# Two heads of a state scan's tail, shifted against each other on TensorE, with quarters of other products between them

## What is computed

```
def step(state, inp):
    r_t, w_t, k_t, v_t, a_t, b_t = inp
    sa = jnp.einsum('bhvk,bhk->bhv', state, a_t)
    state = (state * w_t[:, :, None, :] + sa[..., None] * b_t[:, :, None, :]
             + v_t[..., None] * k_t[:, :, None, :])
    return state, jnp.einsum('bhvk,bhk->bhv', state, r_t)
```

## Time and profile before

| what | value |
|---|---|
| median of 3 runs | 4059.29 us (4054.79 to 4061.07) |
| the profiled execution's own time | 4055.24 us |
| its span, first to last instruction | 4053.5 us |
| mean granted clock of PE | 0.975 of 2.4 GHz |
| PE busy | 3873.0 us, 28244 instructions |
| DVE, ACT, POOL busy | 1954.3, 1635.8, 1652.3 us |
| the sixteen pairs | from some 80 to 512 us and from some 1397 to 1830 us of the span |

### The profile page before, as it was taken

The page is one execution under the profiler, slowest core; times in us unless marked ns, Lnnn a source line. Parts: engine busy times, 40 slices in busy tenths (PEclk is TensorE's granted clock), DMA queues, the critical chain, the costliest instruction groups (busy, mean ns, idle before and its releaser), DMA issues. The chain is left out here.

```text
span 4053.5 us, 67108 instructions
## 1 busy us (share of the span) xinstructions
PE 3873.0 (96%) x28244; PEld 3167.8 (78%) x28244; DVE 1954.3 (48%) x3042; ACT 1635.8 (40%) x2723; POOL 1652.3 (41%) x902
## 2 busy tenths in 40 slices
PE   8999989999999899998899999989999999999998
PEld 6888867878887788886787888777878887787887
DVE  7777673246534777767324654436231123523112
ACT  5554444343334555444434333446233224523222
POOL 4444412434445444441243444534444444444443
PEclk9999999989999899999998999989999999999999
DMA  3111113325532211111332554221222322122332
GB/s 134 48 49 44 67 45 112 104 99 188 186 131 98 85 48 49 44 68 44 111 99 97 193 183 135 99 73 43 98 89 99 98 90 79 53 94 89 99 99 83
DMA packets 108731, 379.52 MB, mean 94 GB/s; under 512 B 12561, under 2 KB 12945, under 8 KB 107793
## 3 DMA queue, kind: packets, MB, share of 16 engines
q1 hardware_dynamic: 98208, 357.27, 25.9%
q10 hardware_dynamic: 10224, 17.97, 1.2%
HBM read 359.46 MB, written 15.73 MB: 93 GB/s over the span
## 5 line engine op out<-in xcount | busy, mean ns | idle before, releaser
L293 POOL TENSOR_TENSOR Wlo<-raw,Whi 128x1024 fp32r<-128x1024 f32 x552 | 1334.4, 2420 | 1995.2 <-ACT Whi L280 1995.0
L228 PE MATMUL ps<-hh,Whi 128*128 128x512 f32 x2864 | 1152.1, 402 | 27.9 <-DVE hl L377 10.1
L228 PE MATMUL ps<-hl,Whi 128*128 128x512 f32 x2864 | 1123.4, 392 | 0.0
L228 PE MATMUL ps<-hh,Wlo 128*128 128x512 f32 x2864 | 1123.2, 392 | 0.0
L280 ACT ACTIVATE Whi<-raw 128x1024 fp32r<-128x1024 f32 x552 | 581.8, 1055 | 708.9 <-PE ps L228 607.9
L228 PEld LDWEIGHTS ps<-hh,Whi 128*128 128x128 f32 x2864 | 542.7, 189 | 160.2 <-issue 28.3
L228 PEld LDWEIGHTS ps<-hl,Whi 128*128 128x128 f32 x2864 | 543.1, 190 | 116.7 <-issue 8.6
L228 PEld LDWEIGHTS ps<-hh,Wlo 128*128 128x128 f32 x2864 | 542.2, 189 | 115.8
L228 PE MATMUL ps<-gh,Whi 128*128 128x512 f32 x864 | 337.6, 391 | 3.8 <-POOL Wlo L293 3.8
L228 PE MATMUL ps<-gh,Wlo 128*128 128x512 f32 x864 | 336.2, 389 | 0.0
L228 PE MATMUL ps<-gl,Whi 128*128 128x512 f32 x864 | 336.1, 389 | 0.0
(11 more groups left out here) (363 smaller groups left out, 5913.6 us busy)
## 6 DMA issues: line engine op xcount, KB each, us to landing
raw<-in_stream SPq DMA_DIRECT2D x554, 512.0 KB, 3.5
ada<-in_ada SPq DMA_DIRECT2D x96, 512.0 KB, 4.6
park_x<-xT SPq DMA_DIRECT2D x2, 2048.0 KB, 7.3
park_yh<-yh ACTq DMA_DIRECT2D x16, 256.0 KB, 2.1
park_yl<-yl ACTq DMA_DIRECT2D x16, 256.0 KB, 2.3
xT<-park_x SPq DMA_DIRECT2D x2, 2048.0 KB, 8.8
yrh<-park_yh ACTq DMA_DIRECT2D x16, 256.0 KB, 8.0
yrl<-park_yl ACTq DMA_DIRECT2D x16, 256.0 KB, 7.9
```

What stands on the lines that cost most here:

```text
L228: last = pe.matmul(ps, left[a](k), right[c](k), start=start and k == 0 and i == 0, stop=stop and k == n - 1 and i == 2)
L293: pool.tensor_tensor(b["Wlo"][:, slot], b["raw"][:, raw_slot(b, u)], b["Whi"][:, slot].bitcast(F32), SUB) \
```

## The change

In the tail, head 1 comes one step behind head 0: U0; then U1 with Z0, block by block; then Z1 with L0, block by block; then L1. Between them stand quarters of r's and k's products: r's last quarter behind U0, and k's first three behind the two mixed groups and behind L1. k's last quarter stays behind S3, and behind S2 there is none. In the inverse, r's first three quarters stand one each behind levels 1, 2 and 3. ACT copies r's result in the tail, between the copies of U0 and U1, and no longer behind level 2. On DVE the state updates S2 and S3 come straight behind RY0 and RY1, and both copies of y behind them. No product is added or dropped, and shapes stay as they are.

```diff
-TAIL_V = Steps("M10", "M11", "M20", "M21", "RY0", "YL0", "RY1", "S2", "YL1", "S3", "Y")
+TAIL_V = Steps("M10", "M11", "M20", "M21", "RY0", "S2", "RY1", "S3", "YL0", "YL1", "Y")
...
+    def u_part(h, c):
+        for u in range(2):
+            last = pe.matmul(b["ps"][half(u), BANK_U + h, c * P:(c + 1) * P], b["XT"][half(u), h, block(c)],
+                             b["AG"][half(u), c, h], start=c == 0, stop=u == 0, skip_group_check=True)
+        if c == BLK - 1:
+            last.then_inc(s["tail_p"], 1)
+
+    def z_part(h, c):
+        last = pe.matmul(b["ps"][half(1), BANK_Z + h, c * P:(c + 1) * P], b["TB"][half(0), h, c, 0, CB:P],
+                         b["Wm"][half(0), h, c], start=True, stop=True)
+        if c == BLK - 1:
+            last.then_inc(s["tail_p"], 1)
+
+    def l_part(h, c):
+        last = pe.matmul(b["ps"][half(1), BANK_U + h, c * P:(c + 1) * P], b["XT"][half(1), h, block(c)],
+                         b["Zs"][half(1), h, c * P:(c + 1) * P], start=False, stop=True, skip_group_check=True)
+        if c == BLK - 1:
+            last.then_inc(s["tail_p"], 1)
+
+    pe.wait_ge(s["tail_a"], TAIL_A(p, "GV"))
+    pe.wait_ge(s["inv_v"], INV_V(p, f"T{LEVELS - 1}0"))
+    for c in range(BLK):
+        u_part(0, c)
+    if p + 2 < PAIRS:
+        rwkv_gemm_pe(pe, s, b, ring, p + 2, "r", 3, 4)
+    else:
+        early_query_pe(pe, s, b, ring, FILL[p, "r"], 3, 4)
+    pe.wait_ge(s["inv_v"], INV_V(p, f"T{LEVELS - 1}1"))
+    pe.wait_ge(s["tail_a"], TAIL_A(p, "U0"))
+    for c in range(BLK):
+        u_part(1, c)
+        z_part(0, c)
+    ahead(0)
+    pe.wait_ge(s["tail_a"], TAIL_A(p, "Z0"))
+    for c in range(BLK):
+        z_part(1, c)
+        l_part(0, c)
     ahead(1)
+    pe.wait_ge(s["tail_a"], TAIL_A(p, "Z1"))
+    for c in range(BLK):
+        l_part(1, c)
+    ahead(2)
     pe.wait_ge(s["tail_a"], TAIL_A(p, "L1"))
...
-        ahead(c + 1)
+        if c == 2:
+            ahead(3)
...
             act.activation(dst[half(u), h], b["ps"][half(u), bank + h], ACT.Copy).then_inc(s["tail_a"], 1)
+            if x == "U" and h == 0:
+                if p + 2 < PAIRS:
+                    rwkv_ev_act(act, s, b, p + 2, "r")
+                else:
+                    early_query_act(act, s, b, FILL[p, "r"])
...
-        if h == 0 and p:
-            dve.wait_ge(s["post_v"], POST_V(p - 1, "yl"))
-        if h:
-            state(1, "S2")
-        dve.tensor_copy(b["y"][vhalf(h)], ps[vhalf(h)]).then_inc(s["tail_v"], 1)
-    state(2, "S3")
+        state(h + 1, f"S{h + 2}")
+    if p:
+        dve.wait_ge(s["post_v"], POST_V(p - 1, "yl"))
+    for h in range(2):
+        dve.tensor_copy(b["y"][vhalf(h)], b["ps"][vhalf(h), BANK_RY + h]).then_inc(s["tail_v"], 1)
...
     dve.wait_ge(s["tail_p"], TAIL_P(p, "Y"))
+    dve.wait_ge(s["tail_v"], TAIL_V(p, "YL1"))
...
-            if l <= 2:
+            if l <= 3:
                 if p + 2 < PAIRS:
-                    rwkv_gemm_pe(pe, s, b, ring, p + 2, "r", l - 1, 2)
+                    rwkv_gemm_pe(pe, s, b, ring, p + 2, "r", l - 1, 4)
                 else:
-                    early_query_pe(pe, s, b, ring, FILL[p, "r"], l - 1, 2)
-            if l == 3:
-                if p + 2 < PAIRS:
-                    rwkv_gemm_pe(pe, s, b, ring, p + 2, "k", 0, 4)
-                else:
-                    early_query_pe(pe, s, b, ring, FILL[p, "k"], 0, 4)
+                    early_query_pe(pe, s, b, ring, FILL[p, "r"], l - 1, 4)
...
-                if p + 2 < PAIRS:
-                    rwkv_ev_act(act, s, b, p + 2, "r")
-                else:
-                    early_query_act(act, s, b, FILL[p, "r"])
```

## The result

The changed kernel takes 4074.83 us (median of 6 runs, 4071.82 to 4078.09), the one before 4057.80 on the same chip (6 runs, 4051.73 to 4061.07): ratio 1.0047, 95% interval 1.0036 to 1.0057, 17.0 us slower. The profiled execution took 4078.09, its span is 4076.3, its mean granted clock 0.972 of 2.4 GHz.

What follows compares the result with a forecast made beforehand. PE, busy 96% of the span, was taken to bound the kernel. 12 x 0.94 + 2 x 2.2 - 2 x 0.78 = +14.1 us on the 4059.3 median gave 4073 us, with 4060 to 4082 for 8 in 10.

Steps and rivals of the forecast that it cites:

- What bounds the kernel, and reading starts: Whole kernel: PE, busy 96% of the span, bounds it; start times were read because short waits do not show.
- Part 1, the shifted heads: Tail: six groups become four, each mixed group taking 0.885 us, a gain of 1.77 us a pair without waits.
- Rival D: Tail: Z0 does not run beside U1, 14.2 us on top of the forecast, 4087 us; chance 0.07.
- Part 2, the quarters between: Tail 1.96 us longer, U0 to M 10.46 instead of 7.02; inverse 2.74 less if PE waits for nothing.
- Part 3, DVE in the tail: Tail: DVE's new order of state updates and y copies costs nothing; S3 some 1.15 us behind S2, as before.
- Part 4, the cover: Inverse levels 1 and 2: POOL's masks delay DVE's row; only 1.02 of 2.74 us kept, +0.94 a middle pair.
- d: Delay of kkr on DVE behind level 1 from POOL's level 4 masks: 1.13 us, bounds 0 and 1.43.
- Rival B: Inverse: masks do not hold DVE up, 2.16 of 2.74 us kept, -1 us in all, 4058; chance 0.18.
- Rival C: Inverse: PE does not wait for the bonus step and exponentials, -0.78 us each pair, 4047; chance 0.12.
- XT stays at about 107.4 ... nothing of the 2.74 is kept, +2.2: First pair of a layer: level 3's XT at about 107.4 against 107.18, so the pair costs 2.2 us more.
- The last pair prepares nothing: -0.78: Last pair of a layer: no preparation for a next pair, so it gains the full 0.78 us.
- 11.3 + 4.4 - 1.6: Sum over 12 middle pairs at +0.94, two first at +2.2 and two last at -0.78: +14.1 us.

Runs made afterwards that it cites:

- old cover, new tail: Changed kernel with r again in halves behind levels 1 and 2, k in eighths, some between the shifted groups: 4046.33 us, ratio 0.9972.
- one-behind-the-other kernel: Changed kernel with mixed groups taken apart, all of U1 then all of Z0, all of Z1 then all of L0: 4091.73 us, ratio 1.0080.
- shift alone: Changed kernel's shifted groups with nothing between them, r and k placed as before the change: 4099.55 us, ratio 1.0105.
- moved masks: Changed kernel with POOL waiting for DVE's kkr before starting level 4's masks: 4062.56 us, ratio 1.0012.
- both mends: Changed kernel with level 4's masks waiting for kkr and no weight unit ahead of U0's copy in the last pair: 4056.52 us, ratio 1.0000.

## Why the prediction held, and where it did not

**What bounds the kernel, and reading starts.** Held. PE alone; what moved was its queue and two of its waits.

**Part 1, the shifted heads.** Held: three quarters and two quarters take 0.885 as forecast, and the shift with cover between is worth 0.86 a pair after the changes of shape (old cover, new tail). Rival D is refuted. The rule beside it, that of the Trainium skill (TensorE: Matmul & The Clock Gate, Part 3, The mechanism), does not hold here either: by that rule a weight load overlaps running products only if its row group differs, so Z0, whose row group U1 is using, would have to take turns with it. The rows at 343.25 and 343.26 and a group of 1.02 us do not agree. The one-behind-the-other kernel corrects the prediction's silent premise, though: nearly half of the overlap (0.39 of 0.885 a group) comes without any written alternation.

**Part 2, the quarters between.** Held to 0.05 us in every middle and first pair (1.91 for 1.96, 10.45 for 10.46).

**Part 3, DVE in the tail.** Held: M to Y is 1.52 shorter (7.32 against 8.84), S2's quarter of 1.48, so DVE's new order costs nothing. (The kernel with the shift alone has that order and S2's quarter in its old place: 8.73.)

**Part 4, the cover.** Held in its mechanism: d is 0.99 for 1.13, and the masks, when they are moved, take 1.00 with them. The order is the one foreseen: first mask, fe, second mask, subtraction, kkr. fe and the subtraction lost 0.49 each, a little less than forecast, and kkr ran free at 0.47. Level 3's XT comes 7.39 behind level 2's W, where 7.6 was forecast (6.5 by B). A middle pair gives +0.72 for +0.94, mostly since kkr was 0.14 earlier. Rival B is the kernel with the moved masks: d = 0, and level 3's XT 2.19 earlier than before (B had 2.16 kept). Rival C is not even reached there, for PE still waits 0.49 for the bonus step; in the changed kernel it waits 1.47.

**The two ends, where the steps failed.** "XT stays at about 107.4 ... nothing of the 2.74 is kept, +2.2": the time of XT was right (107.28), the price was not. It was +4.7 and +4.4, because the 2.24 us without products were followed by nearly 7 us at half clock, a cost that lies behind the wait and not in it. I had priced a wait as its own length. "The last pair prepares nothing: -0.78": it was +1.1. The step left out was the queue of ACT in that pair; I had traced the weight units for the middle pairs and carried the order over, although the last pair's units stand in another. Without the unit in the way the last pair gives -2.63 + 1.84 = -0.8, the forecast.

**The sum.** Forecast 11.3 + 4.4 - 1.6 = 14.1 us; measured in the pairs 8.4 + 9.2 + 2.0 = 19.6, and 17.0 between the medians. The middle pairs' term was too high by 3 and the other two too low by 8. The right direction, and most of the cause, come from the middle pairs; that the total came out within 3 us of the medians' difference is in part luck, since two of its three terms were wrong.

What stays open: why the clock falls in one layer's first pair and not in the other's at the same wait (moved masks: layer 1 and not 0; both mends: layer 0 and not 1). No experiment varied that. Over all the traces the first pairs that wait 2.24 us before level 3's XT have the fall in eight of eight, those that wait 2.05 to 2.08 in two of four, those that wait 1.22 or 0.35 in none of eight.

## What to carry to other kernels

When products are moved from one stage to another, work out first what they covered where they stood: here 2.74 us left the inverse, PE met another engine's row there, and 1.19 was all that came back. Thin cover has two prices beyond the wait: an engine's operations that never met now meet (DVE's and POOL's), and a wait may be followed by several microseconds at half clock. The first and the last turn of a loop have queues of their own, and a good idea (the interleaved groups) is best tried with as little as can be moved around it.

## What the runs showed of the hardware

- Products on different quarters of PE's array run beside each other though they share rows or columns: U1 and Z0 on three quarters in 1.02 us, as long as U0 on two. A free quarter was used ahead of the program's order: with all of U1 written before Z0, Z0's first product started at 347.11, U1's next at 347.20.
- DVE's and POOL's operations on SBUF alone hold each other up: a difference of three columns took 0.66 us beside a mask and 0.17 without, one of 512 columns 1.18 and 0.69, cm 2.31 beside a low part of 2.4. kkr, behind the masks, had its 0.47. It can be POOL that loses: in the first pair after the change two masks beside DVE's dz and v took 2.41 us, in the fifth 1.43.
- After 2.24 us without products the granted clock was 0.51 from 107 to 114 us, and it fell at every wait of this length there (eight of eight); at 2.05 to 2.08 us it fell in two of four, in one layer and not in the other; after 1.22 us it was 1.00; after three waits of 0.7 to 1.3 us with small products between it halved in seven pairs of sixteen (0.52 and 0.50 in the seventh).
